# First stage of a two-layer trunk step: normalising the tokens while they still lie in rows

## The reference, cut to what matters

```python
def rmsnorm(x, g):
    y = x * rsqrt(mean(x * x, axis=-1) + EPS)
    return y * g

def trunk_layer(l, x, cvec, prm, ctx):
    mod = silu(cvec) @ w_mod[l] + b_mod[l]
    shift1, scale1, gate1, shift2, scale2, gate2 = split(mod, 6)
    h = rmsnorm(x, norm_pre[l, 0]) * (1 + scale1) + shift1
    ... even_mixer: h @ ev_w_in, attention and gated DeltaNet, @ ev_w_out
    x = x + gate1 * rmsnorm(mix, norm_post[l, 0])
    ... ConvFFN in the same sandwich; layer 1 has latent attention instead
```

## Time and profile before

| | |
|---|---|
| median of 3 runs | 1928.52 us (1926.64 to 1929.06) |
| profiled execution | 1928.23 us, its span 1926.4 us |
| instructions | 36263 |
| PE busy | 1841.1 us, 96% of the span |
| DVE busy | 963.8 us, 50% |
| ACT busy | 827.9 us, 43% |
| POOL busy | 55.0 us, 3% |
| chain that ended last | PE 85%, DVE 6%, ACT 4%, issue 3%, DMA 1% |
| DMA | 170.23 MB, mean 88 GB/s |

### The profile page before, as it was taken

One profiled execution on the slowest core, in us unless ns is written; L12 is line 12 of the kernel. 1 busy time (PEld: TensorE's weight loads), 2 busy tenths in 40 slices (PEclk: granted clock), 3 DMA queues, 4 the chain that ended last, 5 costly groups with the idle time before them and its releaser, 6 DMA issues.

```text
span 1926.4 us, 36263 instructions
## 1 busy us (share of the span) xinstructions
PE 1841.1 (96%) x14824; PEld 1698.8 (88%) x14824; DVE 963.8 (50%) x1613; ACT 827.9 (43%) x1420; POOL 55.0 (3%) x76
## 2 busy tenths in 40 slices
PE   6999998888899999999999999999999999999998
PEld 3999966667799999999999887776899999999997
DVE  4433355556746655235555743344375553255555
ACT  4545422225745544124445653343464441244453
POOL 0000122220000000000000000000000000000000
PEclk9999999998999999999999999999999999999999
DMA  7222366531021223222234311110211232122243
GB/s 284 65 58 66 128 252 221 199 141 51 1 71 44 77 71 87 71 66 68 73 94 140 95 44 32 27 35 28 67 44 55 76 87 78 55 76 76 78 136 115
DMA packets 238723, 170.23 MB, mean 88 GB/s; under 512 B 20139, under 2 KB 230285, under 8 KB 232333
## 3 DMA queue, kind: packets, MB, share of 16 engines
q1 hardware_dynamic: 238604, 168.54, 28.2%
HBM read 165.08 MB, written 3.44 MB: 87 GB/s over the span
## 4 chain that ended last, share of the span: by engine, by line
PE 85%; DVE 6%; ACT 4%; issue 3%; DMA 1%; SPq 0%; ACTq 0%; DVEq 0%
PE ps L2007 46%; PE ps L2083 15%; PE ps L2040 4%; PE ps L2201 3%; PE ps L2708 2%; PE ps L2745 2%; PE ps L2704 2%; PE ps L2398 1%; PE ps L2220 1%; PE ps L2578 1%; PE ps L2451 1%; PE ps L2555 1%; PE ps L2211 1%; PE ps L2028 1%; ACT w_hi L782 1%
## 5 line engine op out<-in xcount | busy, mean ns | idle before, releaser
L782 ACT ACTIVATE w_hi<-w_raw 128x1024 fp32r<-128x1024 f32 (+4 forms) x187 | 198.6, 1062 | 559.6 <-PE ps L2007 436.0
L1366 DVE TENSOR_TENSOR w_lo<-w_raw,w_hi 128x1024 fp32r<-128x1024 f32 (+4 forms) x191 | 234.2, 1227 | 377.2 <-ACT w_hi L782 376.8
L2007 PE MATMUL ps<-h_hi,w_hi 128*128 128x322 f32 x1648 | 381.5, 313 | 3.2 <-ACT conv L972 1.7
L2007 PE MATMUL ps<-h_lo,w_hi 128*128 128x322 f32 x1648 | 380.2, 312 | 0.0
L2007 PE MATMUL ps<-h_hi,w_lo 128*128 128x322 f32 x1648 | 378.1, 310 | 0.0
L2007 PEld LDWEIGHTS ps<-h_hi,w_hi 128*128 128x128 f32 x1648 | 278.1, 189 | 4.8 <-ACT conv L1192 2.0
L2007 PEld LDWEIGHTS ps<-h_hi,w_lo 128*128 128x128 f32 x1648 | 279.1, 189 | 0.0
L2007 PEld LDWEIGHTS ps<-h_lo,w_hi 128*128 128x128 f32 x1648 | 279.1, 189 | 0.0
L2083 PE MATMUL ps<-g_hi,w_hi 128*128 128x322 f32 x352 | 110.7, 314 | 2.7 <-DVE g_lo L1850 1.6
L2083 PE MATMUL ps<-g_lo,w_hi 128*128 128x322 f32 x352 | 109.6, 311 | 0.0
L2083 PE MATMUL ps<-g_hi,w_lo 128*128 128x322 f32 x352 | 109.1, 310 | 0.0
(11 more groups left out here) (376 smaller groups left out, 3337.5 us busy)
## 6 DMA issues: line engine op xcount, KB each, us to landing
w_raw<-in_ffn_w_up SPq DMA_DIRECT2D x88, 512.0 KB, 3.7
w_mod_raw<-in_w_mod SPq DMA_DIRECT2D x40, 1024.0 KB, 6.9
w_raw<-in_ffn_w_down SPq DMA_DIRECT2D x48, 704.0 KB, 4.5
w_raw<-in_ev_w_in SPq DMA_DIRECT2D x18, 512.0 KB, 3.6
w_mod_first<-in_w_mod SPq DMA_DIRECT2D x8, 1024.0 KB, 15.6
w_raw<-in_ev_w_out SPq DMA_DIRECT2D x8, 512.0 KB, 4.3
w_raw<-in_od_w_out SPq DMA_DIRECT2D x8, 512.0 KB, 4.0
w_raw<-in_od_w_kv_up SPq DMA_DIRECT2D x24, 128.0 KB, 2.3
```

The source lines that it names most:

```text
L782: act.activation(WH[slot][:, 0:k, :], RAW[slot][:, 0:k, :], ACT.Copy).then_inc(w_hi, 1)
L1366: dve.tensor_tensor(WL[slot][:, 0:k, :], RAW[slot][:, 0:k, :], WH[slot][:, 0:k, :].bitcast(F32), ALU.subtract).then_inc(w_lo, 1)
L2007: last = pe.matmul(out, w_of(k, wi), x_of(k, xi, i), start=(k == 0 and p == 0), stop=(k == ks - 1 and p == 2))
```

## The change

The squares are summed on the token rows, where a token is a partition and its sum one number: ScalarE does tiles 0 to 2 (Square with an accumulator), VectorE tiles 3 and 4 (a multiply with a reduction). One Ln and one Exp over five columns give the inverse roots of all tokens. Then every row tile is multiplied with its root into a new tile (`x_unit_rows`, VectorE tiles 0 to 2, ScalarE 3 and 4). PE turns these five first (into XN) and then the five raw tiles (into X), alternately into banks 6, 7 and 2, 3, with six of the eight w_mod pieces set between turns (`MOD_AT`). The sum over channels on PE, the chunks' squares and their sums, and the four multiplications `x_unit` are gone.

ScalarE now issues the five loads of x, ahead of its table load, and later the loads of weight blocks 0 and 1, behind its scaled copies. `hi` and `w_rest` of blocks 0 and 1 stand behind the copies of turns 6 and 8. ScalarE writes h_hi in one step from XN (two instructions a chunk), and VectorE works out the same affine value in fp32 (`x_affine`, two instructions a chunk) to subtract h_hi from it. The gaps of h are zeroed by GpSimd once the last w_mod piece is used. `keep_busy` shrinks from 15 calls to 8 and uses bank 1. The rest of the diff renumbers semaphores.

```diff
+    BY_ACT, BY_DVE, W_AT = (0, 1, 2), (3, 4), (6, 8)
 SP
-            for t in range(NT):
-                src = a["x_prompt"][0] if t == 0 else a["x_sample"][0, (t - 1) * P:t * P, :]
-                sp.dma_start(XR[t][:, :], src).then_inc(S("x_landed"), 16)
...
-            for n in range(23):
+            for n in range(2, 23):
 GpSimd
+            pool.wait_ge(S("mod_done"), KD)
+            zero_gaps(S("gpsimd_filled"), *H2)
 ScalarE
+            for t in range(NT):
+                src = a["x_prompt"][0] if t == 0 else a["x_sample"][0, (t - 1) * P:t * P, :]
+                act.dma_start(XR[t][:, :], src).then_inc(S("x_landed"), 16)
             act.preload_act_table_set("natural_log_exp_and_others")
+            act.wait_ge(S("x_landed"), 16 * NT)
+            for t in BY_ACT:
+                act.activation(XS[t][:, :], XR[t][:, :], ACT.Square, accum_out=XSUM[:, t:t + 1]).then_inc(S("norm_sq"), 1)
...
+            act.activation(XRST[:, 0:NT], XSUM[:, 0:NT], ACT.Ln, scale=1.0 / D, bias=EPSC[:, 0:1]).then_inc(S("norm_ln"), 1)
+            act.wait_ge(S("norm_ln"), 1)
+            act.activation(XRST[:, 0:NT], XRST[:, 0:NT], ACT.Exp, scale=-0.5).then_inc(S("norm_rstd"), 1)
...
+            for t in BY_DVE:
+                act.activation(XS[t][:, :], XR[t][:, :], ACT.Copy, scale=XRST[:, t:t + 1]).then_inc(S("h_shifted"), 1)
+            for n in range(2):
+                act.dma_start(RAW[n][:, 0:KD, :], ein_v[:, :, (6 + n) * P:(7 + n) * P]).then_inc(w_landed[n], 16)
+            for y in range(2 * NT):
+                dst, t = ((XN, X)[y // NT], y % NT)
+                act.wait_ge(S("rows_turned"), 2 * y + 1)
+                act.activation(dst[:, 0:4, TILES[t]:TILES[t] + P], bank((6, 2)[y % 2]).rearrange("p (k c) -> p k c", c=P),
                                ACT.Copy).then_inc(S("rows_copied_a"), 1)
+                if y in W_AT:
+                    hi(W_AT.index(y))
+            act.wait_ge(S("mod_ready"), 1)
+            act.wait_ge(*filled("h_gaps"))
...
             for k in range(KD):
-                act.wait_ge(S("h_scaled"), k // 2 + 1)
                 for c, c0, c1 in CONDS:
-                    last = act.activation(XN[:, k, c0:c1], XN[:, k, c0:c1], ACT.Identity, bias=MOD[0][:, 2 * k + c:2 * k + c + 1],
+                    last = act.activation(Hh[:, k, c0:c1], XN[:, k, c0:c1], ACT.Identity, bias=MOD[0][:, 2 * k + c:2 * k + c + 1],
                                           scale=PA[0][0][:, 2 * k + c:2 * k + c + 1])
-                last.then_inc(S("h_shifted"), 1)
-                act.wait_ge(S("h_shifted"), k + 1)
-                act.activation(Hh[:, k, :], XN[:, k, :], ACT.Copy).then_inc(S("h_hi"), 1)
+                last.then_inc(S("h_hi"), 1)
 VectorE
+            dve.wait_ge(S("x_landed"), 16 * NT)
+            for t in BY_DVE:
+                dve.tensor_tensor_reduce(XS[t][:, :], XR[t][:, :], XR[t][:, :], 1.0, 0.0, ALU.mult, ALU.add, XSUM[:, t:t + 1]
+                                         ).then_inc(S("norm_sum"), 1)
...
+            dve.wait_ge(S("norm_rstd"), 1)
+            for t in BY_ACT:
+                dve.tensor_scalar(XS[t][:, :], XR[t][:, :], XRST[:, t:t + 1], None, ALU.mult).then_inc(S("h_scaled"), 1)
...
+            for y in range(2 * NT):
+                dst, t = ((XN, X)[y // NT], y % NT)
+                dve.wait_ge(S("rows_turned"), 2 * y + 2)
+                dve.tensor_copy(dst[:, 4:8, TILES[t]:TILES[t] + P], q4(bank((7, 3)[y % 2]))).then_inc(S("rows_copied_v"), 1)
+                if y in W_AT:
+                    w_rest(W_AT.index(y))
             dve.wait_ge(S("mod_done"), KD)
             dve.tensor_copy(MROW0[:, :], bank(0)).then_inc(S("mod_rows"), 1)
...
-            w_rest(0)
-            x_unit(3)
-            w_rest(1)
             for k in range(KD):
+                if k >= 2:
+                    dve.wait_ge(S("h_lo"), k - 1)
+                for c, c0, c1 in CONDS:
+                    q = 2 * k + c
+                    step(dve.tensor_scalar(XNA[k % 2][:, c0:c1], XN[:, k, c0:c1], PA[0][0][:, q:q + 1], MOD[0][:, q:q + 1],
+                                           ALU.mult, ALU.add)) if c else dve.tensor_scalar(
...
                 dve.wait_ge(S("h_hi"), k + 1)
-                dve.tensor_tensor(Hl[:, k, :], XN[:, k, :], Hh[:, k, :].bitcast(F32), ALU.subtract).then_inc(S("h_lo"), 1)
+                dve.tensor_tensor(Hl[:, k, :], XNA[k % 2][:, :], Hh[:, k, :].bitcast(F32), ALU.subtract).then_inc(S("h_lo"), 1)
 TensorE
+            MOD_AT = {1: (0,), 2: (1,), 3: (2,), 4: (3,), 6: (4,), 8: (5,)}
...
+            for y in range(2 * NT):
+                t = y % NT
+                if y == 0:
+                    pe.wait_ge(S("h_scaled"), len(BY_ACT))
+                    pe.wait_ge(S("h_shifted"), len(BY_DVE))
+                for part, sem in ((0, "rows_copied_a"), (1, "rows_copied_v")):
+                    if y >= 2:
+                        pe.wait_ge(S(sem), y - 1)
+                    b = ((6, 7), (2, 3))[y % 2][part]
+                    for k in range(4):
+                        last = turn(PS[:, b * 512 + P * k:b * 512 + P * k + P],
+                                    (XS, XR)[y // NT][t][:, (4 * part + k) * P:(4 * part + k + 1) * P])
+                    last.then_inc(S("rows_turned"), 1)
+                for k in MOD_AT.get(y, ()):
+                    first_mod(k)
+            first_mod(KD - 2)
+            keep_busy(1, 2)
+            first_mod(KD - 1)
+            keep_busy(1, 1)
             mod_turn(1, MROW0, 5)
...
-            keep_busy(6, 12)
+            keep_busy(1, 5)
             first_pair(0)
```

More of the change, by code:

```diff
@@ L127, in S @@
         return sems[name]
-    NORMS = (("first", KD, 1), ("l2", 8, 8), ("on", 4, 8), ("cq", C_Q // P, 1), ("ckv", C_KV // P, 1))
+    BY_ACT, BY_DVE, W_AT = (0, 1, 2), (3, 4), (6, 8)
+    NORMS = (("first", 0, 0), ("l2", 8, 8), ("on", 4, 8), ("cq", C_Q // P, 1), ("ckv", C_KV // P, 1))
     CHUNKS = {name: k for name, k, _ in NORMS}
@@ L143, in of @@
             base = sum(k for name, k, s in before if s == 1 and not name.startswith("pre"))
-        return S(f"norm_{kind}"), base + n
-    FILLED = ("eps", "qkv_edges", "od_gaps", "o_attn_gaps", "g_edges0", "g_edges1")
+        return S(f"norm_{kind}"), base + n + {"sq": len(BY_ACT), "sum": len(BY_DVE), "ln": 1, "rstd": 1}.get(kind, 0)
+    FILLED = ("eps", "h_gaps", "qkv_edges", "od_gaps", "o_attn_gaps", "g_edges0", "g_edges1")
     def filled(name):
@@ L237, in build @@
     VR = [place(f"vec_rows{b}", [P], R_T + P * b) for b in range(4)]
+    XS = [place(f"x_unit_rows{t}", [D], R_W + D * t) for t in range(NT)]
+    XNA = [place(f"x_affine{s}", [TW], R_A + al(TW) * s) for s in range(2)]
+    XSUM = place("x_row_sum", [8], R_SC)
+    XRST = place("x_row_rstd", [8], R_SC + 8)
     SCX = place("silu_c", [KD, 32], R_SCS)
@@ L505, in next_weights @@
         return RESH[x], RESL[x]
-    H0, HP0 = KD, KD // 2
+    H0, HP0, HS0 = KD, len(BY_ACT), len(BY_DVE)
+    RT0, RC0 = 4 * NT, 2 * NT
     SUB = ((0, 0), (0, 1), (1, 0), (1, 1))
@@ L1507, in gains @@
                     VC[:, v0:v0 + 8].unsqueeze(2).broadcast_to([P, 8, 2]), op, ALU.mult), signal)
+            for x in XNA:
+                dve.memset(x[:, 0:1], 0.0)
+                dve.memset(x[:, P0 + PROMPT:S0], 0.0)
+                dve.memset(x[:, S0 + SAMPLE:TW], 0.0)
             dve.memset(X[:, :, 0:1], 0.0)
@@ L2236, in _, with first_mod @@
                 turn(PS[:, 4 * 512 + 128 * b:4 * 512 + 128 * b + n], VR[b][0:n, :], n).then_inc(S("vec_turned"), 1)
-            pe.wait_ge(S("x_landed"), 16 * NT)
-            for t in range(NT):
-                for part, sem in ((0, "rows_copied_a"), (1, "rows_copied_v")):
-                    if t:
-                        pe.wait_ge(S(sem), t)
-                    for k in range(4):
-                        last = turn(PS[:, (6 + part) * 512 + P * k:(6 + part) * 512 + P * k + P],
-                                    XR[t][:, (4 * part + k) * P:(4 * part + k + 1) * P])
-                    last.then_inc(S("rows_turned"), 1)
-            pe.wait_ge(S("silu_c"), 1)
-            for k in range(KD):
-                if k == KD - 2:
-                    norm_stat("first")
+            MOD_AT = {1: (0,), 2: (1,), 3: (2,), 4: (3,), 6: (4,), 8: (5,)}
+            def first_mod(k):
+                if k == 0:
+                    pe.wait_ge(S("silu_c"), 1)
                 pe.wait_ge(S(f"mod_landed{k}"), 16)
                 mod_part(MWS[k], k, 0)
-            keep_busy(6, 3)
+            for y in range(2 * NT):
[17 more added lines that the diff above has]
+            keep_busy(1, 1)
             mod_turn(1, MROW0, 5)
+            pe.wait_ge(S("rows_copied_a"), RC0)
+            pe.wait_ge(S("rows_copied_v"), RC0)
             H = (Hh, Hl)
-            keep_busy(6, 12)
+            keep_busy(1, 5)
             first_pair(0)
```

58 lines of the change are left out of this document (22 added, 36 removed).

## The result

| | before | after |
|---|---|---|
| median of 22 executions each, same chip, us | 1929.6 (1924.35 to 1934.49) | 1934.27 (1927.31 to 1939.06) |
| profiled execution, us (span) | 1928.23 (1926.4) | 1933.68 (1931.9) |
| first product of `first_pair`, us | 45.86 | 44.54 |
| block 2's product, us | 62.10 | 60.78 |

The ratio is 1.0023, 95% interval [1.0014, 1.0033]: 4.4 us slower. 1926.6 was forecast, with 1922.6 to 1929.8 as the range; 1934.27 lies outside of it. Yet the first stage is shorter, by 1.3 us instead of the 1.9 forecast. So 5.8 us (1.32 + 0.0023 x 1929) were lost behind it, where nothing was forecast.

A forecast was written before the change was run, and what follows sets the result against it. PE, busy 96% of the span, was taken as the bound, so only the first product's start counted: 45.86 to 44.0 us, 1.9 us saved. Off the median 1928.52 that gave 1926.6 us, range 1922.6 to 1929.8.

The forecast's parts named there:

- (a): Loading x at the start: issued by ScalarE from about 0.75, its last tile lands at 13.1 instead of 14.33 us.
- rival A: Loading x: w_mod pieces stand behind x, which lands at 10.4, 2.7 us earlier; total 1923.9 us; chance 0.30.
- Rival B: Loading x: w_mod overtakes it, x lands at 15.7, first product at 46.6; total 1929.2 us; chance 0.11.
- The weighed rule: DMA engines round-robin between queues by the packet, so w_mod would cut into x; result 2.6 us worse than forecast.
- (b): Statistics and scaling on ScalarE and VectorE, between x's landing and the first transpose: 6.8 us of new serial work.
- (c): PE's transposes and w_mod pieces, up to the last piece: 20.1 us, ending at 40.0 where it was 37.8.
- rival C: Weight blocks 0 and 1 starve behind w_mod, block 0 landing at 35; costs 1.7 us, total 1928.3; chance 0.06.
- (d): From the last w_mod piece to the first product of `first_pair`: 4.0 us against 8.06.
- (e): Pace of `first_pair`: VectorE needs about 1.6 us a chunk, PE 1.71, so PE stays the bound and 0 is lost.
- the first part: What bounds the whole kernel: PE's chain of matmuls, so a first product d earlier ends the kernel d earlier.

The follow-up runs named there:

- after_wearly: The changed kernel with ScalarE issuing the loads of weight blocks 0 and 1 right behind x, not behind its scaled copies; 1932.99 us, ratio 1.0015.
- after_rawfirst_pad: The changed kernel with raw tiles turned first, blocks 0 and 1 in SP's list, and 72 plus 37 small transposes added on PE; 1928.8 us, ratio 0.9989.

## Why the prediction was wrong

By its steps:

(a) x at 11.1, between the forecast 13.1 and rival A's 10.4. Rival B did not happen. The weighed rule was right and my use of it wrong: w_mod didn't overtake x, since the vectors' small rows stood ahead of it in SP's list. The queues from 5 to 10 us, x in q10, vectors in q1 (the first row of w_mod, 8192 B, starts at 10.23):

```profile
q10 hardware_dynamic: 516, 1.90, 92.8%
q1 hardware_dynamic: 362, 0.15, 10.6%
```

x lost almost no bytes to them. The vectors were late for it (PE turned them at 11.8 instead of 7.2), off the path.

(b) 6.2 us against 6.8: right. VectorE's multiplication of 1024 columns took 0.748 (at most 0.89 was said), ScalarE's 1.15.

(c) 23 us from the first turn to the end of the last piece, against 20.1. The granted clock was 1.00 throughout, as said. Turn 9 took from 34.3 to 37.2 instead of 1.0 us, with PE waiting for ScalarE's and VectorE's copies behind block 0; that is 1.9 of the 2.9 us too many, and without the wait after_wearly was 2.7 earlier. Most of the rest is in the turns themselves, 1.0 us each where 0.8 was taken. The wait was rival C, which I gave 0.06 and 1.7 us. Its landing was foreseen there (35; it was 33.6), but the forecast's own sum took the blocks as landed by turn 6, at 1.5 us each, as if they came whole in order of issue. That is the failed step of the first stage: bytes don't go in order between two lists. The Trainium skill, DMA: Bandwidth & Descriptors, "Queues, rings and completion order", has the engines take turns between queues by the packet. I had weighed this for x and not for the blocks, where it decides.

(d) 4.2 us from the last piece to the first product, against 4.0; (e) a chunk of VectorE 0.34 + 0.54 + 0.83 = 1.71, PE 13.65 as before, so PE stayed the bound. Both right.

The sum of the first stage: 1.3 instead of 1.9. With that alone, 1927.2 would have been well inside the range.

The step that failed was in the first part: "Nothing in between is bound to a clock time", so "a first product that starts d earlier ends the kernel d earlier". No load or wait is bound to a time, that held (1.32 ahead at 62 us, 1.3 at 225). But the borders of the program's pages are bound to a count of instructions, and the change adds 46. I had charged these only with their own time. 5.8 us were lost behind the first stage; about 4 of them went away when the count was made whole again, and the other 2 stay open. The prediction had named the sign of its being wrong: "if anything behind 62 us, shifted, differs by more than a microsecond". The rows were in the trace of before ("issue" pieces of 0.8 to 1.7 us in the chain at 243 to 380, and queue q8), but I read the chain only to 120 us.

In the profiled pair a part of the difference from 225 to 430 us is the partner: before had no low clock there, as the only one of the fourteen profiled. It had 17.1 us from 440 to 457 instead, where the others have 0 to 6.8. The ratio of 22 executions each doesn't rest on this pair.

## What to carry to other kernels

Count the instructions that a change adds to PE's program, modulo 256, and look for "issue" pieces in the chain far behind the edit: where matmuls are short, a shift of 46 cost 4 us here, more than the edit gained. To tell a real gain in one stage from such a shift, pad the count back in an idle place and compare stage by stage, not by the total. And a load of short rows doesn't share the DMA engines by bytes with one of long rows in another list: put it in the same list, at the place where it is needed.

## What the runs showed of the hardware

- PE's program is fetched in 16 KB packets, one per 247 PE instructions from 225 to 470 us (the view has fewer elsewhere); the stalls lie at one place of the page, were 0.5 to 2.5 us where exposed, and ended 2.2 to 2.6 us after the packet's start.
- Of 27 such stalls of 1.9 us or more 21 were followed by the lower granted clock, for 3.4 us or longer; of 53 under 1.6 us, 4 were.
- Two DMA lists take turns packet for packet: 864 to 866 packets while the bytes stand 6.29 to 0.44 MB.
- 16-column transposes cost 0.065 us each on a PE that is running (37 in 2.40 us in after_rawfirst_pad), 0.109 on one that has just started (72 in 7.85 us).
